# Multiplying six pairs of U blocks of the second half inside the first gate round, and closer gate teams in the last quarter

## What is computed

```python
def block(args):
    xt, it, gt = args
    act = jax.nn.gelu(jnp.einsum('td,ted->te', xt, u_tab[it]), approximate=False)
    return jnp.einsum('te,ted->td', gt * act, v_tab[it])
```

## Time and profile before

| | |
|---|---|
| median of 3 timed runs | 1494.44 us (1493.45 to 1495.6) |
| span of the profiled execution | 1510.1 us |
| busy: PE, DVE, POOL, ACT | 1357.4, 1167.1, 661.0, 381.7 us |
| bytes moved | 444.25 MB, 294 GB/s over the span |

### The profile page before, as it was taken

The page is one execution under the profiler, slowest core; times in us unless marked ns, Lnnn a source line. Parts: engine busy times, 40 slices in busy tenths (PEclk is TensorE's granted clock), DMA queues, the critical chain, the costliest instruction groups (busy, mean ns, idle before and its releaser), DMA issues.

```text
span 1510.1 us, 18614 instructions
## 1 busy us (share of the span) xinstructions
PE 1357.4 (90%) x6418; PEld 951.5 (63%) x6418; DVE 1167.1 (77%) x2515; ACT 381.7 (25%) x769; POOL 661.0 (44%) x548
## 2 busy tenths in 40 slices
PE   8999989999999997776999799999799999999940
PEld 6787755788888885554444355588688874444410
DVE  5836345778888898769877899989888888666688
ACT  4233010111111011169210345556431110000010
POOL 2244111042343345600455464635365675665572
PEclk9999999999999997875899899999899999999975
DMA  6411422365888889930699999989799999999995
GB/s 230 146 57 56 158 88 98 132 223 179 326 336 345 347 310 399 405 111 1 232 416 412 389 393 354 415 337 391 259 382 381 414 413 414 413 414 413 414 357 208
DMA packets 118285, 444.25 MB, mean 294 GB/s; under 512 B 11568, under 2 KB 24368, under 8 KB 101808
## 3 DMA queue, kind: packets, MB, share of 16 engines
q0 software_dynamic: 73728, 268.47, 46.2%
q1 hardware_dynamic: 43888, 173.56, 29.8%
q10 hardware_dynamic: 576, 1.05, 0.2%
HBM read 440.93 MB, written 2.10 MB: 293 GB/s over the span
## 4 chain that ended last, share of the span: by engine, by line
PE 51%; DMA 15%; DVE 14%; POOL 5%; issue 5%; ACT 4%; DVEq 3%; ACTq 1%; SPq 0%
PE ps L1246 31%; DMA big<-in_peer_v_dram,idx 13%; PE ps L1263 7%; PE ps L1299 6%; DVE y L1085 4%; POOL big L568 3%; POOL big L558 2%; DVE big L1064 2%; ACT wr L608 2%; DMA big<-in_peer_u_dram,idx 2%; ACT wr L610 1%; PE ps L1473 1%; PE ps L1405 1%; ACTq L609 1%; PE ps L1432 1%
## 5 line engine op out<-in xcount | busy, mean ns | idle before, releaser
L558 POOL DMA_INDIRECT big<-in_peer_u_dram,idx x256 | 311.2, 1216 | 571.6 <-DVE dots L1064 455.5
L1085 DVE SCALAR_TENSOR_TENSOR y<-big,wgt,y 128x1024 f32<-128x1024 f32 x256 | 328.3, 1282 | 47.5 <-DMA big<-in_peer_v_dram,idx 36.9
L1064 DVE CUSTOM_DVE_ANT_0 big<-big,xh 128x1024 f32<-128x1024 f32 x256 | 311.7, 1224 | 61.3 <-DMA big<-in_peer_u_dram,idx 29.7
L568 POOL DMA_INDIRECT big<-in_peer_v_dram,idx x256 | 288.8, 1128 | 116.6 <-issue 70.9
L1246 PE MATMUL ps<-xT,big 128*128 128x256 f32 x1024 | 231.5, 385 | 11.0 <-issue 10.9
L1299 PE MATMUL ps<-big,pool_mem 128*128 128x512 f32 x512 | 226.5, 598 | 0.0
L1246 PEld LDWEIGHTS ps<-xT,big 128*128 128x128 f32 x1024 | 196.6, 193 | 40.8 <-issue 14.3
L1299 PEld LDWEIGHTS ps<-big,pool_mem 128*128 128x128 f32 x512 | 97.5, 192 | 120.0 <-issue 120.0
L1299 PE MATMUL ps<-y,pool_mem 128*128 128x512 f32 x256 | 116.8, 608 | 0.8 <-DVEq L1221 0.8
L1246 PE MATMUL ps<-xT,y 128*128 128x256 f32 x512 | 115.5, 384 | 0.0
L1246 PE MATMUL ps<-xT 128*128 128x256 f32 x512 | 114.6, 382 | 0.0
(11 more groups left out here) (226 smaller groups left out, 1479.2 us busy)
## 6 DMA issues: line engine op xcount, KB each, us to landing
big<-u_pairs_dram SPq DMA_DIRECT2D x32, 1024.0 KB
big<-v_pairs_dram SPq DMA_DIRECT2D x32, 1024.0 KB
y<-u_pairs_dram SPq DMA_DIRECT2D x16, 1024.0 KB
xT<-u_pairs_dram SPq DMA_DIRECT2D x16, 1024.0 KB
y<-v_pairs_dram SPq DMA_DIRECT2D x16, 1024.0 KB
xT<-v_pairs_dram SPq DMA_DIRECT2D x16, 1024.0 KB
big<-in_w_in_dram SPq DMA_DIRECT2D x24, 512.0 KB, 5.8
pool_mem<-in_peer_w_q_dram SPq DMA_DIRECT2D x12, 1024.0 KB
```

The costliest lines, as they stand in the source:

```text
L558: nc.gpsimd.indirect_dma_start(urow[n % RING], None, peer_u2, bass.IndirectOffsetOnAxis(ap=idx[:, u, e:e + 1], axis=0)).then_inc(s_u[n % R ...
L568: nc.gpsimd.indirect_dma_start(vrow[n % RING], None, peer_v2, bass.IndirectOffsetOnAxis(ap=idx[:, u, e:e + 1], axis=0)).then_inc(s_v[n % R ...
L1064: V.tensor_tensor_reduce(out=urow[n % RING], in0=urow[n % RING], in1=xh[:, u // PH * D:(u // PH + 1) * D], scale=1.0, scalar=0.0, op0=ALU. ...
L1085: V.scalar_tensor_tensor(acc_rows[t], vrow[n % RING], wgt[:, u % 2, e:e + 1], acc_rows[t], ALU.mult, ALU.add).then_inc(s_vadd, 1)
```

## The change

Six pairs of U blocks of half 1 (k = 0 to 5) leave stage 4 and are multiplied in the gate round: after each of the 32 groups PE does 3 of their 96 matmuls (`EARLY_STEP`, new job kind `early`). ACT writes their gelus into free memory (`early_acts`: a part of `xh` that is not in use then and 4 KB per partition of new memory `spare_acts`), and DVE multiplies them with the gates at rows 141 to 146. `sequence` puts the six pairs into the order of the loads behind the U pairs of half 0. In the round the gate groups now use banks 4 and 5, the early pairs 6 and 7. In stage 4 the 16 teams (1, 1) now stand in front of the 10 pairs 6 to 15. On DVE they stand at rows 141 to 157 (9/8 rows apart), products 6 to 15 at rows 144 to 161, and 16 to 31 at rows 162 to 191. Gelus of the gathered rows move in ACT's list: unit 8 from behind pair 3 to behind pair 9, 9 from 10 to 17, 10 from 19 to 25, 11 from behind pair 27 to the start of stage 5. The memory that POOL's transfers use for their descriptors is halved, which makes room for `spare_acts`.

```diff
+EARLY = 6
+EARLY_STEP = 16 * EARLY // GROUPS
...
-    return [first + m * 15 // 8 for m in range(TEAMS)]
+    return [first + (m * 9 // 8 if s else m * 15 // 8) for m in range(TEAMS)]
...
-    return [k for k in range(HALF // 2) if n == team_rows(1, 1)[0] + (k + 2) * 15 // 8]
+    first = team_rows(1, 1)[0]
+    after = [k if k < EARLY else 2 + (k - EARLY + 1) * 9 // 5 if k < TEAMS else 20 + (k - TEAMS + 1) * 15 // 8
+             for k in range(HALF // 2)]
+    return [k for k in range(HALF // 2) if n == first + after[k]]
+
+def sequence(r, n):
+    if n < HALF:
+        return 2 * HALF * r + n if r == 0 or n >= 2 * EARLY else HALF + n
+    return 2 * HALF * r + n + (2 * EARLY if r == 0 else 0)
...
-        for n in range(HALF // 2):
+        first = EARLY if r == 1 else 0
+        for n in range(first, HALF // 2):
             if r == 1 and n < TEAMS:
-                add("team", 1, 1, n, by="act")
-                if n + 1 < TEAMS:
-                    jobs.append(("onehot", (1, n + 1), None))
+                share = TEAMS - EARLY
+                for m in range((n - first) * TEAMS // share, (n - first + 1) * TEAMS // share):
+                    add("team", 1, 1, m, by="act")
+                    if m + 1 < TEAMS:
+                        jobs.append(("onehot", (1, m + 1), None))
...
     def gate_round():
+        waiting = []
         for n in range(GROUPS):
             jobs.append(("half", (n,), None))
+            while waiting and waiting[0] <= EARLY_STEP * (n - 1):
+                add("act", 1, waiting.pop(0) // 16 - 1, by="dve")
             add("gate", n, by="dve")
+            jobs.append(("early", (n,), None))
+            if EARLY_STEP * (n + 1) // 16 > EARLY_STEP * n // 16:
+                waiting.append(EARLY_STEP * (n + 1) // 16 * 16)
+        for done in waiting:
+            add("act", 1, done // 16 - 1, by="dve")
...
+                elif kind == "act" and arg[1] < EARLY:
+                    A.activation(early_acts[arg[1]], bank, ACT.Gelu).then_inc(free[b], 1)
+                    A.drain().then_inc(s_early, 1)
...
+                if kind == "early":
+                    for m in range(EARLY_STEP * arg[0], EARLY_STEP * (arg[0] + 1)):
+                        n_, q, k = m // 16, m // 8 % 2, m % 8
+                        b, n = BANK["act", 1, n_]
+                        if q == 0 and k == 0:
+                            pe.wait_ge(free[b], n)
+                        cols = block_of(1, 2 * n_ + q).rearrange("p (k n) -> p k n", k=KC)
+                        last = T.matmul(ps[:, b, q * DENSE:(q + 1) * DENSE], cols[:, k, :], hT[:, 1, k, :],
+                                        start=(k == 0), stop=(k == KC - 1))
...
-    nc = _bacc.Bacc("TRN2", target_bir_lowering=False, num_devices=1, dynamic_dma_scratch_size=8192)
+    nc = _bacc.Bacc("TRN2", target_bir_lowering=False, num_devices=1, dynamic_dma_scratch_size=4096)
```

More of the change, by code:

```diff
@@ L40, in products_after @@
 def products_after(n):
-    return [k for k in range(HALF // 2) if n == team_rows(1, 1)[0] + (k + 2) * 15 // 8]
+    first = team_rows(1, 1)[0]
[6 more added lines that the diff above has]
+    return 2 * HALF * r + n + (2 * EARLY if r == 0 else 0)
+SEQUENCE = sorted((sequence(r, n), r, n) for r in range(2) for n in range(0, 2 * HALF, 2))
 def chosen_before(n):
@@ L211, in static_jobs @@
     dense_first_half(1)
-    dense_second_half(1, range(12, GUNITS))
+    dense_second_half(1, range(11, GUNITS))
     placed, used, n_front, n_score, n_late = [], [0] * 8, 0, 0, 0
@@ L215, in static_jobs @@
     for i, (kind, arg, by) in enumerate(jobs):
-        if kind in ("split", "norm", "scale", "gelu", "gates", "expert", "onehot", "half"):
+        if kind in ("split", "norm", "scale", "gelu", "gates", "expert", "onehot", "half", "early"):
             placed.append((kind, arg, by, None, None))
@@ L230, in static_jobs @@
             b = 4 + arg[0]
+        elif kind == "gate":
+            b = 4 + arg[0] % 2
+        elif kind == "act" and arg[0] == 1 and arg[1] < EARLY:
+            b = 6 + arg[1] % 2
         elif scoring and not late:
@@ L378, in layer @@
         gateT = [work[:, 256:512], work[:, 0:256]]
+        early_acts = [xh[:, GATHERED * D + 512 * k:GATHERED * D + 512 * k + 512] for k in range(4)] + [
+            spare_acts[:, 512 * k:512 * k + 512] for k in range(EARLY - 4)]
         ps = ctx.enter_context(nc.psum_tensor("ps", [P, 8, 512], f32))
@@ L507, in load_pair @@
                 sp.dma_start(dring[p % DPAIRS], src).then_inc(s_blk[p % DPAIRS], 16)
-            for p in range(HALF):
+            for p in range(HALF + EARLY):
                 load_pair(p)
@@ L513, in _ @@
             sp.dma_start(lnp2[:, 1, :], ln2_b[0].partition_broadcast(P)).then_inc(s_ln, 16)
-            for p in range(HALF, 2 * HALF):
+            for p in range(HALF + EARLY, 2 * HALF):
                 load_pair(p)
@@ L598, in _ @@
                     A.activation(acc_rows[t], xh[:, t * D:(t + 1) * D], ACT.Copy, scale=ALPHA).then_inc(s_y, 1)
+                    continue
+                if kind in ("early", "expert"):
                     continue
@@ L1155, in gated_gelu @@
                     dve.wait_ge(s_gx, n // TEAMS + 1)
-                dve.wait_ge(s_gl, n + 1)
                 x3 = X[:, 2 * n:2 * n + 2, :]
+                if n < EARLY:
+                    dve.wait_ge(s_early, n + 1)
+                    V.tensor_tensor(x3, early_acts[n].rearrange("p (i n) -> p i n", i=2), x3, ALU.mult
+                                    ).then_inc(s_earlyd, 1)
+                    return
+                dve.wait_ge(s_gl, n - EARLY + 1)
                 V.tensor_tensor(x3, ps[:, b, :].rearrange("p (i n) -> p i n", i=2), x3, ALU.mult).then_inc(free[b], 1)
@@ L1278, in block_of @@
             def block_of(r, n):
-                b_ = 2 * HALF * r + n
-                pair, side = divmod(b_, 2)
+                pair, side = divmod(sequence(r, n), 2)
                 pe.wait_ge(s_blk[pair % DPAIRS], 16 * (1 + pair // DPAIRS))
@@ L1288, in _ @@
                     continue
+                if kind == "early":
[7 more added lines that the diff above has]
+                                        start=(k == 0), stop=(k == KC - 1))
+                        if q == 1 and k == KC - 1:
+                            last.then_inc(full[b], 1)
+                    continue
+                if kind == "act" and arg[0] == 1 and arg[1] < EARLY:
+                    continue
                 if kind == "expert":
@@ L1292, in _ @@
                         pe.wait_ge(s_wgtd, 1)
-                    if i % 2 == 0 and r == 1:
+                    if i % 2 == 0 and r == 1 and i // 2 < EARLY:
+                        pe.wait_ge(s_earlyd, i // 2 + 1)
+                    elif i % 2 == 0 and r == 1:
                         b, n = BANK["act", 1, i // 2]
```

8 lines of the change are left out of this document (5 added, 3 removed).

## The result

| | median us | runs | span of the profiled execution |
|---|---|---|---|
| before | 1493.95 (1488.96 to 1495.6) | 4 | 1510.1 (first), 1492.5 (second) |
| changed | 1518.49 (1515.33 to 1522.3) | 4 | 1517.8 |

The ratio is 1.0156, 95% interval 1.0141 to 1.0172: the change costs 24.5 us. The forecast was 1507.5, which is +13, with a range to 1515.5. The sign was right, the size was not, and the range was too narrow.

A forecast was written before the change was run, and what follows sets the result against it. Transfers at their 413 GB/s limit were taken to bound the kernel, with ACT pacing the gate round. Terms +9.3 (round), -15.2 (bytes) and +19 (lost transfers) gave +13 on 1494.4, so 1507.5 us, range 1486 to 1515.5.

The forecast's parts named there:

- its walk through the rows: PE, ACT and DVE followed through the teams (1, 1) to row 255: row 191 at 1222 us, sum +15 us.
- The signs that it named as right ones: Groups 2.35 to 2.45 us, clock near 1.00, six ACT waits, row 158 over 35 us later, last V about 10 earlier.
- What bounds the kernel: Transfers at their limit, 413 GB/s, in the last stretch; ACT sets the gate round's pace; PE doesn't set the end.
- The rival that PE sets the end: At the end, time goes with PE's last V block, 1450 to about 1440: -10 us (1484.5); chance 0.05.
- Term 1: Gate round: PE needs about 2.38 us a group against ACT's 2.07 and becomes the bound; +9.3 us.
- costed at nothing: Product 0's wait for a team copy (2.5 us), lost cover of free banks, smaller descriptor memory: no net cost.
- The rival from the Trainium skill: Gate round: 16 small matmuls cost 0.4 us, so it grows by 2 us only; +6 us (1500); chance 0.08.
- Term 2: Bytes: six pairs loaded in the gate round, where nothing else moves, 6 x 2.54 us; -15.2 us.
- Term 3: Rows 141 to 191: 48 us of transfers lost instead of 28.7, from ACT waits at six double teams; +19 us.
- Waits for PE's gelus, 7.5 us before, add about 5: Rows 158 to 191: DVE's gelu waits add about 5 us to 125 us of DVE work.
- I take 1.4 us for each of the six: Double teams: after each wait for ACT, slower PE matmuls on a dipped clock cost 1.4 us.
- The faster rival: Rows 141 to 191: teams run at DVE's pace, double-team waits below about 1 us; -9 us (1485.5); chance 0.13.

The follow-up runs named there:

- run 6: The kernel before with 15/16 of the bytes of six of the last 32 V pairs not loaded: 1480.15 us against 1495.8, ratio 0.9901.
- run 7: The kernel before with 41 us of PE's V matmuls left out and all loads kept: 1496.87 us, ratio 1.0005.
- run 8: The changed kernel with two one-hot buffers and only two of each early block's eight matmuls: 1487.97 us against 1494.38, ratio 0.9952.
- run 3: The changed kernel with a second buffer for ACT's one-hots and descriptor memory of 2048 bytes: 1495.21 us, ratio 1.0001 to before.
- run 5: The changed kernel with one buffer, the second team of each double put between the pair's two U blocks: 1498.03 us, ratio 1.0019 to before.
- run 4: The kernel before with a second buffer for ACT's one-hots and descriptor memory of 4096 bytes: 1494.49 us against 1494.38, ratio 0.9993.
- run 11: The changed kernel with two early pairs, two one-hot buffers and teams 13/8 rows apart: 1498.22 us, ratio 1.0021 to before.
- runs 12 and 13: The changed kernel with two early pairs, two buffers, teams 15/8 rows apart; in 13 products some four rows sooner: ratios 1.0129 and 1.0112 to before.
- runs 1 to 11: The first eleven follow-ups, from the kernel before profiled again unchanged (1494.39 us) to the change with two early pairs and two buffers (1498.22 us).
- runs 12 to 14: Two early pairs, two buffers, two product placings (1529.32, 1528.83 us); then the kernel before with closer teams, two buffers, no early pairs (1510.12 us).
- run 12: The changed kernel with two early pairs, two buffers, teams 15/8 rows apart, product 2 at row 148: 1529.32 us against 1509.75, ratio 1.0129.

## Why the prediction was right in sign and too small

**The sums side by side.** "Measured" is the changed kernel's profile against the second one of before. The prediction has two sums, one of terms and one of its walk through the rows. They don't cut the time in the same way: in the second line the term counts us of transfers lost, the walk the growth of the stretch.

| | terms | walk | measured |
|---|---|---|---|
| gate round, seen at row 80 | +9.3 | +9 | +10.8 |
| rows 80 to 141 | 0 | 0 | +2.0 |
| rows 141 to 191 | +19 (lost) | +22 | +26.6 (lost: 28.1) |
| row 191 to the end | -15.2 | -16 | -14.1 |
| sum | +13 | +15 | +25.3 |

The signs that it named as right ones came: groups 2.35 us apart, a granted clock of 0.95 in the round, waits for ACT at six double teams, row 158 45 us later, 413 GB/s in the last stretch.

**What bounds the kernel: right.** Taking bytes away pays (-15.7 us in run 6) although PE's last V block ends where it did; taking PE's work away pays nothing (run 7). The rival that PE sets the end is out. PE's last V block ends at 1426.3 instead of 1433.0 (forecast: about 10 us earlier), and the time doesn't follow it.

**Term 1: right mechanism, 1.5 us short.** A group takes 2.35 us (forecast 2.38) and PE is the bound; run 8 takes three quarters of the early matmuls out and gets 7.2 us back. The first two groups cost 2 us more than the rest: PE had been idle for 19.09 us, and its large matmuls ran slower. The prediction took the clock at the start of the round as 1.00 from the earlier trace rows, but there PE had waited only 2.46 us; that wait stands in the first execution alone. So the round is 11.3 us longer than in the second profile of before (10.8 as row 80 sees it). Against the first profile's 68.9 us it would be 8.1: what was short here is as much the base as the sum.

Between rows 80 and 141 another 2.0 us go. They are product 0, which now stands at row 141: it waits 1.50 us for ACT's last copy of a team (1, 0) and takes 0.61 itself, ahead of the row. The prediction had such a wait under "costed at nothing", as what product 0 lost before at row 144 (2.6 us in the second profile). In run 3 the wait is 2.3 us and the stretch 3.0 us longer.

The rival from the Trainium skill (TensorE: Matmul & The Clock Gate, "Back-to-back issue gap") is out: 16 small matmuls take 0.98 us before the next large one starts, not the 0.4 that follows from its figure, and the round grew by over 10 us and not by 2. The page gives that figure for isolated matmuls and says itself that at few columns it counts too little where weights are loaded in between.

**Term 2: right.** -14.1 here, -16.7 in run 3, -15.7 in run 6.

**Term 3: this is the step that failed, by its size.** The cause holds: "six times, 25 us" of waits for ACT's single buffer were measured as 24.3 us at the six double teams, and with a second buffer (run 3) or 3.5 us of matmuls between the teams (run 5) 20 to 23 us come back. But 56.8 us of transfers are lost between rows 141 and 191, not 48. What was mis-sized is DVE's waiting between rows 158 and 191.
- "Waits for PE's gelus, 7.5 us before, add about 5". I put only the growth of 5 on 125 us of pure work and left the 7.5 out. DVE waited 10.4 us for gelus and 3.4 for rows there, and the stretch took 136.1 us instead of 130, though the work in it came to some 122 us and not 125.
- "I take 1.4 us for each of the six" dips of the clock was too low as well: the pairs behind the waits took 8.71 to 9.89 us instead of 7.15, 1.6 to 2.7 each, 14 us in all instead of 8.4. My one row for it, 5.10 us against 3.5, held only 8 records of V; a pair behind a wait has 32. This did not make the walk short, though. Counted from row 141, pair 15 ends at 130.4 us on PE, forecast 130.3, and the last pair of U at 240.9, forecast 240.8. The first team came some 3 us sooner than forecast (it ends 4.0 us after row 141 starts, forecast 7.1), which made up for a good part of the dips. That was luck.

The walk up to row 158 was good: 111 us forecast (113 by its own times 979 and 1092), 110.8 measured. So the sum came short behind it: rows 141 to 191 take 246.9 us, not 242, and 190.1 us of transfers are carried in them, not 193.5. I also had two results, +13 from the terms and +15 from the walk, and took the lower. The range's top, +21, left no room for the gelu waits: at 13.8 us instead of 5 they alone would have taken the walk's +15 to +24.

**What was costed at nothing.** The descriptor memory of 4096 bytes was nothing together with the buffer (run 4). Product 0's wait was 1.5 us, as told above.

**The faster rival** (waits under 1 us, -9) can be seen in run 3: the waits are gone, and the result is 0, not -9. It would have failed by 2 us up to row 141, and because rows 141 to 191 take 3.3 us more than before, where I had them 3 shorter.

**Which version is best?** None beats the kernel before. With ACT's chain hidden, six early pairs bring 16.7 us behind row 191 and cost 11.5 up to row 141 and 3.3 among the teams (run 3). With two early pairs the round is free, but what the bytes bring, 7.3 us behind row 191, is lost among the teams (run 11). Whether products placed between those of runs 12 and 13 would keep them is open.

## What to carry to other kernels

When a schedule puts two users of a single-buffered product next to each other, the producer's whole chain (here copy, eight one-hots, relu: 4.75 us) becomes a wait each time. A second buffer, or the halves of other work between the two, is worth more than what the closer schedule was made for. Price a wait of PE with the slower matmuls behind it over the whole piece of work that follows. When you put waits on a sum of pure work, put all of them on it and not their growth over before; and carry a walk through to its end rather than adding a lump. Before you rest a sum on a profile whose span is a per cent above the timed runs, profile the same kernel again: which waits have no releaser tells where it was disturbed.

## What the runs showed of the hardware that I had not expected

The kernel before took 1494.4 to 1495.8 us (medians) on the three chips of runs 1 to 11, and 1509.75 and 1511.74 us (medians of 11 and 17 runs) on the two of runs 12 to 14. The profiles of runs 12 to 14 show what the first profile of before shows: PE's matmuls ahead of the gate round come late without a releaser. So what I took for an odd execution may be an ordinary one of such a chip. More of PE's waits from 560 to 1250 us in run 12:
```profile
PE ps L1291 <- issue: 11.4, 9, 2.2
PE ps L1520 <- ACT wr L646: 10.7, 20, 2.5
PE ps L1359 <- issue: 5.9, 3, 2.7
PE ps L1507 <- issue: 4.0, 3, 2.2
```
The transfers are at their limit in that stretch (409 GB/s from 573 to 590 us of the first profile of before); that PE's instructions come late because of them was only thought of, not shown.

After 19 us of idleness PE's first large matmuls took 2.90 us for six records, at a granted clock of 0.50, the second six 2.20, and from the third group on, at 1.00, 1.53. The small f16 matmuls between them took the same 1.15 to 1.17 us for 16 all the time, at the granted 0.50 of the round before as at the 0.95 of the change: here their pace doesn't follow the clock.
